# A fused two-block model on one NeuronCore: the projection's weight pieces land where their low halves will stand, in a ring of five, and the late units are dealt out differently

## The reference, cut to what matters

```python
mod_x = (silu(c)     @ w_ada + b_ada)      # six rows of 2048: sh1, s1, g1, sh2, s2, g2
mod_c = (silu(c_ctx) @ w_ada + b_ada)      # only sh1c, s1c are used
h  = modulate(rmsnorm(x),   sh1,  s1)      # 256 tokens
hc = modulate(rmsnorm(ctx), sh1c, s1c)     # 256 context tokens
p  = h @ w_in                              # w_in: 2048 x 3776; k, v and the kv latent also for hc
q_da, k_da, v_da = p[:, :1024], p[:, 1024:2048], p[:, 2048:3072]
c_q  = rmsnorm(p[:, 3072:3456]);  q_mla = c_q @ w_uq     # 384 x 1536
c_kv = rmsnorm(p[:, 3456:3712]);  kv    = c_kv @ w_ukv   # 256 x 2048, for hc too
x = x + g1 * (attention(...) @ w_o)        # then an FFN with sh2, s2, g2, then the second block
```

## Time and profile before

| | us |
|---|---|
| time, median of 3 runs (2905.98 to 2922.33) | 2907.97 |
| the profiled execution's own time | 2909.04 |
| its span in the trace | 2907.3 |
| mean granted TensorE clock, 1 = full | 0.987 |
| PE busy over the span | 2795.1 (96%) |
| the projection from piece 8 on | 142.99 to 448.30 |

### The profile page before, as it was taken

The page is one execution under the profiler, slowest core; times in us unless marked ns, Lnnn a source line. Parts: engine busy times, 40 slices in busy tenths (PEclk is TensorE's granted clock), DMA queues, the critical chain, the costliest instruction groups (busy, mean ns, idle before and its releaser), DMA issues.

```text
span 2907.3 us, 34135 instructions
## 1 busy us (share of the span) xinstructions
PE 2795.1 (96%) x13474; PEld 2284.7 (79%) x13474; DVE 1748.6 (60%) x1859; ACT 1228.3 (42%) x1343; POOL 161.2 (6%) x267
## 2 busy tenths in 40 slices
PE   6969899999999999999999999999999999999998
PEld 3657776687888888888888888888788888888887
DVE  2574677875655555555765567985755455545454
ACT  3222226644444334435465443434644444434333
POOL 0011030100000000000000000015300000000000
PEclk9989999999999999999999999999999999999999
DMA  9886886784545565546757776666366555555554
GB/s 396 316 310 214 306 298 215 257 301 145 188 160 190 196 220 188 173 163 210 225 192 252 244 225 218 225 192 202 88 197 210 190 196 189 176 189 202 167 174 151
DMA packets 348572, 621.29 MB, mean 214 GB/s; under 512 B 50304, under 2 KB 102672, under 8 KB 340896
## 3 DMA queue, kind: packets, MB, share of 16 engines
q1 hardware_dynamic: 311568, 586.63, 59.6%
q10 hardware_dynamic: 36880, 32.94, 3.4%
HBM read 590.51 MB, written 29.00 MB: 213 GB/s over the span
## 4 chain that ended last, share of the span: by engine, by line
PE 86%; DVE 5%; DMA 4%; issue 2%; ACT 2%; SPq 0%; POOL 0%; ACTq 0%; DVEq 0%; POOLq 0%
PE ps L309 23%; PE ps L311 23%; PE ps L310 23%; DMA raw<-in_w_ada 3%; PE ps L1249 2%; PE ps L1251 2%; PE ps L1250 2%; DVE X L1153 1%; PE ps L427 1%; PE ps L1528 1%; DVE w_lo L271 1%; DVE w_lo L975 1%; PE ps L1919 1%; PE ps L1481 1%; DMA ada_b<-in_pack_ada 1%
## 5 line engine op out<-in xcount | busy, mean ns | idle before, releaser
L271 DVE TENSOR_TENSOR w_lo<-raw,w_hi 128x2048 fp32r<-128x2048 f32 (+3 forms) x428 | 896.7, 2103 | 672.9 <-ACT w_hi L264 671.7
L264 ACT ACTIVATE w_hi<-raw 128x2048 fp32r<-128x2048 f32 (+3 forms) x428 | 747.3, 1757 | 735.7 <-PE ps L311 682.7
L309 PE MATMUL ps<-w_hi,a_hi 128*128 128x512 f32 x2240 | 876.9, 391 | 3.4 <-DVE a_lo L803 2.7
L311 PE MATMUL ps<-w_hi,a_lo 128*128 128x512 f32 x2240 | 872.2, 389 | 0.0
L310 PE MATMUL ps<-w_lo,a_hi 128*128 128x512 f32 x2240 | 871.7, 389 | 0.0
L309 PEld LDWEIGHTS ps<-w_hi,a_hi 128*128 128x128 f32 x2240 | 420.6, 188 | 90.4 <-DVE a_lo L803 3.3
L311 PEld LDWEIGHTS ps<-w_hi,a_lo 128*128 128x128 f32 x2240 | 420.5, 188 | 87.8
L310 PEld LDWEIGHTS ps<-w_lo,a_hi 128*128 128x128 f32 x2240 | 420.7, 188 | 85.4
L309 PE MATMUL ps<-w_hi,b_hi 128*128 128x512 f32 x796 | 312.2, 392 | 3.5 <-DVE b_lo L842 3.5
L311 PE MATMUL ps<-w_hi,b_lo 128*128 128x512 f32 x796 | 310.5, 390 | 0.0
L310 PE MATMUL ps<-w_lo,b_hi 128*128 128x512 f32 x796 | 310.5, 390 | 0.0
(11 more groups left out here) (372 smaller groups left out, 2671.3 us busy)
## 6 DMA issues: line engine op xcount, KB each, us to landing
raw<-in_hyb_w_in SPq DMA_DIRECT2D x96, 1024.0 KB, 5.7
raw<-in_sc_w_in SPq DMA_DIRECT2D x96, 1024.0 KB, 5.1
raw<-in_w_up SPq DMA_DIRECT2D x88, 1024.0 KB, 5.0
raw<-in_w_ada SPq DMA_DIRECT2D x96, 512.0 KB, 5.9
raw<-in_w_down SPq DMA_DIRECT2D x48, 768.0 KB, 4.3
raw<-in_w_in SPq DMA_DIRECT2D x24, 1024.0 KB, 7.2
raw<-in_hyb_w_out SPq DMA_DIRECT2D x32, 768.0 KB, 4.5
raw<-in_sc_w_out SPq DMA_DIRECT2D x32, 768.0 KB, 4.4
```

What stands on the lines that cost most here:

```text
L264: nc.scalar.activation(w_hi[s][:, 0:n_k, 0:ncols], raw[s][:, 0:n_k, 0:ncols], ACT.Copy).then_inc(sem("hi_done"), 1)
L271: nc.vector.tensor_tensor(w_lo[s][:, 0:n_k, 0:ncols], raw[s][:, 0:n_k, 0:ncols], w_hi[s][:, 0:n_k, 0:ncols].bitcast(F32), ALU.subtract).th ...
L309: nc.tensor.matmul(o, h, w_hi[s][:, k, 0:ncols], start=kt == 0, stop=False)
L311: last = nc.tensor.matmul(o, l, w_hi[s][:, k, 0:ncols], start=False, stop=kt == L.groups[-1][0] + L.groups[-1][1] - 1)
```

## The change

1. The weight of piece p now lands at the place of its low half, and DVE's subtraction writes over it. There are five such slots (`PROJ_RING`): the four pairs `w_hi`/`w_lo`, and `raw0` (high) with `raw1` (landing and low) as the slot of pieces with p % 5 = 2.
2. `proj_load` of piece p waits until PE has used piece p-5 (was: until DVE had split p-2). `proj_hi` waits for the landing alone.
3. SP's order becomes: load of piece p, then the loads of the late units behind piece p-1 (was: load of p+2, then those behind p).
4. `LATE_AFTER` has other numbers and KL's transposes move one piece later in `LAT_AT`, and with them DVE's evictions.

```diff
-        LATE_AFTER = [0] * 7 + [3, 0, 3, 3, 3, 5, 5, 5, 5, 1, 2, 1, 2, 2, 2, 2, 2, 0, 1, 0, 1, 6, 6, 6, 6, 1, 1, 1, 2, 5, 5, 5, 4]
+        LATE_AFTER = [0] * 7 + [4, 2, 2, 2, 3, 1, 1, 2, 1, 5, 5, 5, 5, 2, 2, 2, 1, 1, 0, 1, 1, 5, 5, 5, 5, 2, 2, 2, 2, 5, 5, 5, 5]
-        LAT_AT = {10: (0, 1), 11: (2,), 14: (3, 4), 15: (5, 6)}
+        LAT_AT = {10: (0, 1), 11: (2,), 15: (3, 4), 16: (5, 6)}
...
         def proj_load(sp, p):
             src, n_k, ncols = piece(p)
-            if p >= RAW_PROJ:
-                sp.wait_ge(sem("lo_done"), p - RAW_PROJ + 1)
-            sp.dma_start(raw[p % RAW_PROJ][:, 0:n_k, 0:ncols], src).then_inc(sem(f"landed{p % RAW_PROJ}"), 16)
+            if p == 3:
+                sp.wait_ge(sem("flip_t"), KT)
+            if p == 4:
+                sp.wait_ge(sem("ada_used"), ADA_IN_X)
+            if p >= RING:
+                sp.wait_ge(sem("hi_done"), p - RING + 1)
+            if p >= PROJ_RING:
+                sp.wait_ge(sem("piece_used"), p - PROJ_RING + 1)
+            sp.dma_start(landing[p % PROJ_RING][:, 0:n_k, 0:ncols], src).then_inc(sem(f"landed{p % RING}"), 16)
+
+        raw_01 = [place(f"raw_r{i}", [P, GROUP, CHUNK], F32R, at=base + i * PIECE_BYTES) for i in range(2)]
+        landing = [place(f"landing{i}", [P, GROUP, CHUNK], at=a) for i, a in enumerate(
+            (W0 + 4 * PIECE_BYTES, W0 + 5 * PIECE_BYTES, base + PIECE_BYTES, W0 + 6 * PIECE_BYTES, W0 + 7 * PIECE_BYTES))]
+        slots = [(w_hi[0], w_lo[0]), (w_hi[1], w_lo[1]), (raw_01[0], raw_01[1]), (w_hi[2], w_lo[2]), (w_hi[3], w_lo[3])]
...
-            for p in range(FIRST_PIECES - RAW_PROJ - 1, N_PROJ):
-                if p + RAW_PROJ < N_PROJ:
-                    proj_load(sp, p + RAW_PROJ)
+            for p in range(FIRST_PIECES - 1, N_PROJ):
+                proj_load(sp, p)
                 if p in ATT_FIRST:
                     att_first_sp(sp, ATT_FIRST.index(p))
-                for n in units_after(p):
+                for n in units_after(p - 1):
                     if n + LATE_SLOTS < N_UNITS:
                         late_load(sp, n + LATE_SLOTS)
...
-            if p >= RING:
-                act.wait_ge(sem("piece_used"), p - RING + 1)
-            nc.scalar.activation(w_hi[s][:, 0:n_k, 0:ncols], raw[p % RAW_PROJ][:, 0:n_k, 0:ncols], ACT.Copy
+            hi, w = proj_slot(p)[0], landing[p % PROJ_RING]
+            act.wait_ge(sem(f"landed{p % RING}"), 16 * (p // RING + 1))
+            nc.scalar.activation(hi[:, 0:n_k, 0:ncols], w[:, 0:n_k, 0:ncols], ACT.Copy
                                  ).then_inc(sem("hi_done"), 1)
```

More of the change, by code:

```diff
@@ L261, in split_hi @@
             s = p % RING
-            act.wait_ge(sem(f"landed{s}"), at(16 * (p // RING + 1 - LAND0[s]), i, step * 16 // RING))
+            act.wait_ge(sem(f"landed{s}"), at(16 * (p // RING + 1), i, step * 16 // RING))
             act.wait_ge(sem("piece_used"), at(p - RING + 1, i, step))
@@ L937, in proj_sp @@
                 late_load(sp, n)
-            for p in range(FIRST_PIECES - RAW_PROJ - 1, N_PROJ):
-                if p + RAW_PROJ < N_PROJ:
-                    proj_load(sp, p + RAW_PROJ)
+            for p in range(FIRST_PIECES - 1, N_PROJ):
+                proj_load(sp, p)
                 if p in ATT_FIRST:
                     att_first_sp(sp, ATT_FIRST.index(p))
-                for n in units_after(p):
+                for n in units_after(p - 1):
                     if n + LATE_SLOTS < N_UNITS:
                         late_load(sp, n + LATE_SLOTS)
-            sp.wait_ge(sem("lo_done"), N_PROJ)
+            for n in units_after(N_PROJ - 1):
+                if n + LATE_SLOTS < N_UNITS:
+                    late_load(sp, n + LATE_SLOTS)
+            sp.wait_ge(sem("piece_used"), max(p for p in range(N_PROJ) if p % PROJ_RING == 2) + 1)
             gate_bias_load(sp, 0)
@@ L968, in proj_lo @@
             _, n_k, ncols = piece(p)
[L969 to L973, removed]
+            (hi, lo), w = proj_slot(p), landing[p % PROJ_RING]
             dve.wait_ge(sem("hi_done"), p + 1)
-            nc.vector.tensor_tensor(w_lo[s][:, 0:n_k, 0:ncols], raw[p % RAW_PROJ][:, 0:n_k, 0:ncols],
-                                    w_hi[s][:, 0:n_k, 0:ncols].bitcast(F32), ALU.subtract).then_inc(sem("lo_done"), 1)
+            nc.vector.tensor_tensor(lo[:, 0:n_k, 0:ncols], w[:, 0:n_k, 0:ncols],
+                                    hi[:, 0:n_k, 0:ncols].bitcast(F32), ALU.subtract).then_inc(sem("lo_done"), 1)
         def proj_pair(c):
@@ L1239, in proj_piece @@
                 pe.wait_ge(sem("lo_done"), p + 1)
[L1240 removed]
+            w, w_low = proj_slot(p)
             for k in range(n_k) if steps is None else steps:
@@ L1248, in proj_piece @@
                         h, l = hi(kt, t), lo(kt, t)
-                        nc.tensor.matmul(o, h, w_hi[s][:, k, 0:ncols], start=kt == 0, stop=False)
-                        nc.tensor.matmul(o, h, w_lo[s][:, k, 0:ncols], start=False, stop=False)
-                        last = nc.tensor.matmul(o, l, w_hi[s][:, k, 0:ncols], start=False, stop=kt == groups[-1][0] + groups[-1][1] - 1)
+                        nc.tensor.matmul(o, h, w[:, k, 0:ncols], start=kt == 0, stop=False)
+                        nc.tensor.matmul(o, h, w_low[:, k, 0:ncols], start=False, stop=False)
+                        last = nc.tensor.matmul(o, l, w[:, k, 0:ncols], start=False, stop=kt == groups[-1][0] + groups[-1][1] - 1)
             if k == n_k - 1:
```

11 lines of the change are left out of this document (3 added, 8 removed).

## The result

The changed kernel took 2893.07 us in the median of 10 runs (2886.15 to 2902.11), the kernel before 2914.70 us in 10 runs beside them (2905.98 to 2922.33). The ratio is 0.993 with a 95% interval of 0.9915 to 0.9945: 16 to 25 us faster. The profiled execution took 2895.72 us (span 2893.9, mean clock 0.987). Lines have shifted: L1249 to L1251 are L1255 to L1257 now, L1100 L1106, L1114 L1120, L975 L981, L964 L974, L1153 L1159, L1165 L1171; in the three kernels that send the loads first they stand two further down.

What follows compares the result with a forecast made beforehand. PE, busy over the span, was taken as the bound, with 46.5 us of waits and low clock behind them to win. 15.5 + 0.6 + 1.2 + 3.8 + 0.9 + 1.0 = 23.0; 2909.0 - 23.0 = 2886 us, range 2864 to 2907.

Steps and rivals of the forecast that it cites:

- The main term: Units and transposes, pieces 8 to 16: KL's scaling no longer waits for 15 units, 15.5 us gained.
- The scaling and the transposes: Pieces 8 to 16: PE's waits 1.0 + 3.5 + 0 + 8.0 = 12.5 us instead of 28.0.
- the walk: DVE and PE timed step by step over pieces 10 to 17: KL's scaling at 189.6, last eviction at 207.9.
- I take 6.3 where few late loads are in flight: Weight loads in the short pieces: 6.3 us to landing, against 6.9 elsewhere.
- 8.8 us for five units: DVE behind a low half: five late units take 8.8 us, the mean of 9.7 and 7.8.
- The ring: New slots and load order, same splits and bytes: counted at nothing in long pieces, a loss in short ones.
- The third rival: Projection: the weight load becomes the path, at 12 us per load 2924 us, slower than before; chance 0.08.
- signs of the wrong: Projection: weight loads over 9 us, DVE waiting for ACT or PE waiting in V0 or V1, over 2 us at pieces 8 to 10.
- V0 and `uk`: V0 without waits; the first late row's total, moved to piece 20, covers one wait ahead of `uk`: 1.2 us.
- K1: Pieces 28 to 31, five units instead of six: waits 5.7 instead of 9.5 us, 3.8 gained, 0.9 of clock.
- Q1 and V1: Two units each behind pieces 32 to 35: waits about as before (4 us), 1.0 us gained by the clock.
- The clock: PE runs at low clock after long waits; fewer such stretches: 0.6, 0.9 and 1.0 us gained.

Runs made afterwards that it cites:

- middle_only: The kernel before with only the late units behind pieces 12 to 19 exchanged (1, 1, 2, 2, 5, 5, 5, 5), old `LAT_AT`: ratio 0.9912.
- ring_only: The changed kernel with the old `LATE_AFTER` and `LAT_AT`, keeping the ring of five and SP's new order: ratio 1.0007.
- loads_first: The changed kernel with the weight load of piece p+1 sent ahead of the late loads behind piece p-1: ratio 0.9875.
- out_later: The changed kernel with DVE taking over the first late row two pieces later: ratio 0.9925.
- evict_early: The changed kernel with DVE's evictions of the latent transposes, and ACT's high halves of them, one piece sooner: ratio 0.9908.
- lf_lat_old: `loads_first` with the old `LAT_AT` (KL's transposes at pieces 14 and 15): ratio 0.9864, median 2868.45 us.
- numbers_only: The kernel before with the change's `LATE_AFTER` and `LAT_AT`, on the old rings: ratio 0.9896, run again 0.9890.
- lf_all: `lf_lat_old` with the line of `out_later`: ratio 0.9847, median 2869.67 us.

## Why the prediction was right, and where it was not

The predicted time of 2886 us is 7 us below the measured median, and the range holds it. The predicted gain of 23.0 us lies in the measured 16 to 25. Of the 7 us 5.7 are the base: 2909.0 was the profiled execution, 2907.97 a median of three, and ten runs gave 2914.70. The other 1.4 are the gain, 21.6 between the medians. The main term and its mechanism are right. That the sum comes so close is in part luck: 3.1 us fewer of waiting were saved than forecast, and some 6 us, by an estimate, go with a higher clock instead of 2.5 (below). In the profiled pair the terms are these.

**The scaling and the transposes, right.** Forecast: 12.5 us of waits instead of 28.0. Measured: 11.9. The transposes (3, 4) wait for nothing, as forecast, and (5, 6) 6.71 us (forecast 8.0). QL's first transposes, forecast to wait 1.0, wait for nothing, and QL's last wait 5.16 us instead of 3.5: piece 12's low half came 0.8 us later than forecast, and PE was there 0.9 us sooner. `middle_only` shows that dealing out units anew behind 12 to 19 does this without the ring.

**Two sizes in the walk were wrong and cancelled.** The step "I take 6.3 where few late loads are in flight" failed: the median landing of pieces 12 to 16 was 7.7 us, in the whole stage 8.0 (chain above). Piece 12's low half was at 169.3 instead of 168.5, KL's scaling at 191.8 instead of 189.6, the low half of 15 at 194.5 instead of 192.5, that of 16 at 199.4 instead of 196.0. But 8.8 us for five units, the mean of the earlier trace rows, was too long as well. Four blocks had landed when the units began, and the fifth, asked for at 200.67 when the first unit had left its slot, landed in 3.3 us. Before, the fifth blocks behind pieces 14 and 15 took 7.2 and 5.2 us, sent 1.2 us behind a 1 MB weight load each time; here the weight load ahead was sent 4.5 us earlier. So DVE did not wait:

```profile
197.15 2.29 DVE L981 TENSOR_TENSOR w_lo<-landing,w_hi 128x2048 fp32r<-128x2048 f32 x1 [1.45 <-ACT w_hi L974]
199.36 6.06 DVE L1159 SCALAR_TENSOR_TENSOR X<-raw,condf,X 128x1024 f32<-128x1024 f32 x5
205.34 2.28 DVE L981 TENSOR_TENSOR raw_r<-landing,raw_r 128x2048 fp32r<-128x2048 f32 x1
207.54 0.87 DVE L1120 TENSOR_SCALAR lat_f<-ps,col 128x256 f32<-128x256 f32 x2
```

The eviction ended at 208.4, forecast 207.9.

**The ring, "alone I count it at nothing in long pieces and a loss in the short ones", right.** `ring_only` is 1.0007. That the loss could be bought back by the order of two statements on SP (16 us, `loads_first`) stands nowhere in the prediction: the price was in the walk, and the remedy beside it was not looked for. The rule quoted there, issue a DMA early and wait for it late ("DMA: Bandwidth & Descriptors", Rules for kernel authors, of the Trainium skill), is what `loads_first` does; the trace agrees in the direction. Its price does not: an estimated 4.4 us by that page's fit (Anatomy of one DMA; the page states it for DMAs that GpSimd issues, and SP issues these), 6.1 to 8.1 measured.

**The third rival, half right.** "The load becomes the path" is what the chain shows in Q0's short pieces. In V0's long ones the landing stayed below the 9.2 us at which it was to decide (5.8 to 8.0 for pieces 17 to 19), and PE had no wait there; the share of the DMA engines from 209.60 to 254.22 us was 0.89, forecast above 0.8. Two signs of the wrong did show later on: the loads of pieces 29 and 36 took 9.6 and 9.3 us, and PE waited 2.31 us in V1.

**V0 and `uk`, 1.2 us gained, wrong.** The step was that the total of the first late row would cover one wait ahead of `uk`. It did cover one (three waits of 1.16 instead of three of 1.16 and one of 1.65), but the stretch from the end of V0 to the end of `ur` grew from 40.48 to 50.41 us. 4.7 us of it are the total itself, moved in (3.3 moved out of V0). The rest, 5.2 us, nobody had counted: PE's busy time beside the total grew by 3.9 us, at a clock of 0.90 instead of 1.00, and idle time by 1.4. The total ran at a low clock, piece 20 behind it took 7.7 us instead of 5.7, and the pieces behind the wait of 2.99 us 1.9 more than before. The total:

```profile
254.22:258.93 4.71, 4.71 (x33) 4.70 (x32) 0.00 (x0) 1.02 (x1) 0.00 (x0) 0.73 0.91 324
```

And DVE, in its program order, waited 5.24 us for the total with V0's eviction behind it; from there the copies, the stores and the high halves into `uq` ran late (2.99 us at 296.57). `out_later` shows this chain, and that taking it away gives little: K1 is held by the load of piece 28, sent at 298.08 behind a unit of piece 26 and landed at 305.33. That the low clock comes from the new place of the total isn't shown: `evict_early` has it in the same place, at a clock of 0.98 and in 3.63 us.

**K1, right in sum.** Forecast 5.7 us of waits instead of 9.5, measured 5.10: at piece 28 5.10 (forecast 4.0), at piece 30 none (forecast 1.7). The clock gave 2.0 us there (45.82 busy instead of 47.82), forecast 0.9.

**Q1 and V1, wrong sign.** Forecast: waits equal, clock 1.0 better. Measured: 5.6 us of waits instead of 3.9, busy time 1.2 longer. Of the three (2.42, 0.90, 2.31) the first two stand behind the groups of two units of Q1's pieces, which had 1, 1, 1 and 2 before; that these groups are the cause isn't shown.

**The clock.** I put 2.5 us down to fewer low stretches. Busy time over the projection at the same matmuls went from 258.77 to 263.26 us with the mean clock at 0.93 in both. So 17.4 us fewer of waiting bought no clock at all in this pair. Over many executions the clock is higher. The profiled ones both have a mean clock of 0.987 over the whole kernel. But the 39 executions of the kernel before that ran beside the experiments have 0.9856 in the mean, and the ten of the change 0.9880. Eleven of the 39 have 0.987 like the profiled one, and took 2911.0 us in the mean; the four of the change with 0.987 took 2895.2. That is 15.8 us at the same clock; the other 6 us of the 21.6 go with the higher clock, an estimate from executions run at different times. The forecast had 2.5.

## What to carry to other kernels

When work is dealt out over a pipeline, count units per microsecond of the engine that waits, not per piece: eight numbers were worth 25 us, the new ring by itself nothing. A load that is due next goes ahead of loads that are due later on the same queue; a ring makes room for an early load but doesn't send it. A small product that another engine picks up in program order (a total of 3.6 us) can hold up what is queued behind the pick-up: moving it brought V0's eviction 5.3 us and K1 2.8 us forward, though the time didn't show it.

## What the runs showed of the hardware

- A 1 MB weight load took 6.1 to 7.4 us to landing in the median of each of the six profiles with the rings of before, and 7.7 to 8.1 in the eight with the ring of five. In these eight a weight load is sent 0.4 to 0.7 us behind the load before it (20 of 20 in the change, 19 of 20 in `loads_first`), in the six mostly 2 us or more behind it. The share of the DMA engines was 0.83 after, 0.78 before.
- What goes with the landing time is how much is still in flight when the load is sent. Over all 14 profiles (280 loads of 1 MB) the median is 6.0 us with 0.5 MB or less of earlier weight and late loads under way, 7.2 with 1 MB, 7.5 with 1.5, 8.2 with 2 and 8.7 with more. In the mean there were 1.0 to 1.3 MB under way with the rings of before, and 1.5 to 1.7 with the ring of five.
- The total of a late row, 32 matmuls of 128 x 2 with no wait ahead, takes 3.63 us at full clock. That of the first row took so long in `before`, `middle_only`, `evict_early`, `lf_lat_old` and `numbers_only`, but 4.68 when `numbers_only` was run again, and 4.84 after, 4.37 in `lf_all`, 4.34 in `ring_only` and 4.05 in `loads_first`; the stretch of it in the profile after has a clock of 0.73. The clock can fall in work that never stops, and does so in some executions of a kernel and not in others.
- Two profiled executions differed by 13.3 us where the medians of ten differed by 21.6. Terms of a few microseconds that rest on the clock can't be told from one pair.
